# Normalisation of mixers B and C: ScalarE's three operations over two steps, the product on GpSimd

## The reference, cut to what matters

```python
p = jax.nn.softmax(sc, axis=-1)
return jnp.einsum('bhqs,bshd->bqhd', p.astype(v.dtype), v)
```

## Time and profile before

| | |
|---|---|
| time, median of 3 executions | 2663.72 us (2663.42 to 3135.05) |
| profiled execution | 2675.02 us |
| its span on the slowest core (core 0) | 2673.4 us |
| spans of the 8 cores | 2654.1 to 2673.4 us |
| mean granted TensorE clock, core 0 | 0.980 of full speed |
| PE busy | 2548.5 us (95%) |
| DVE busy | 1085.5 us (41%) |
| ACT busy | 1038.7 us (39%) |
| POOL busy | 278.4 us (10%) |
| B and C pairs, layer 0 | about 203 to 579 us |
| B and C pairs, layer 1 | about 1509 to 1876 us |

### The profile page before, as it was taken

How to read it: one execution, slowest core, us unless ns; L and a number is a source line. 1 busy time by engine, 2 the same in 40 slices (tenths; PEclk the granted TensorE clock), 3 DMA queues, 4 the chain that set the end, 5 groups by cost and what they waited for, 6 DMA issues and landing times.

```text
span 2673.4 us, 41394 instructions; the slowest of 8 cores (2654.1 to 2673.4 us)
## 1 busy us (share of the span) xinstructions
PE 2548.5 (95%) x15104; PEld 1234.8 (46%) x15104; DVE 1085.5 (41%) x1612; ACT 1038.7 (39%) x1398; POOL 278.4 (10%) x340
## 2 busy tenths in 40 slices
PE   3889999989999999999999999999999999999997
PEld 1335556544444444444443455565444444444443
DVE  1544434444444414132265444344444462322326
ACT  2567776662223410101154677757222252011012
POOL 2410000000001210000120100000000020000002
PEclk8999999999999999999999999999999999999998
DMA  9304221202234343433331011121122332222214
GB/s 195 66 16 77 49 40 22 63 13 36 42 51 122 65 81 52 71 64 64 87 112 29 16 18 21 22 59 25 24 43 42 75 93 46 40 40 39 41 24 126
DMA packets 66516, 148.01 MB, mean 55 GB/s; under 512 B 6592, under 2 KB 19456, under 8 KB 64272
## 3 DMA queue, kind: packets, MB, share of 16 engines
q0 software_dynamic: 55712, 99.76, 23.5%
q1 hardware_dynamic: 10608, 45.61, 5.1%
HBM read 228.12 MB, written 16.97 MB: 92 GB/s over the span
## 4 chain that ended last, share of the span: by engine, by line
PE 90%; DVE 3%; issue 3%; DMA 2%; ACT 2%; DVEq 0%; POOL 0%; ACTq 0%; POOLq 0%; SPq 0%
PE ps L381 73%; PE ps L379 16%; DMA sb_WS<-wada 1%; DVE sb_OS L410 1%; ACT sb_RD L391 1%; ACT sb_PT L391 1%; DMA sb_XT<-x 0%; DMA sb_WS<-win 0%; DVE sb_W L404 0%; DVE sb_XT L400 0%; DVE sb_TMPF L400 0%; DVE sb_RD L395 0%; ACT sb_HT L391 0%; DVE sb_W L410 0%; DMA sb_WS<-wfi 0%
## 5 line engine op out<-in xcount | busy, mean ns | idle before, releaser
L381 PE MATMUL ps<-sb_HT,sb_WS 128*128 128x512 bf16 (+1 forms) x5760 | 1331.0, 382 | 25.5 <-ACT sb_HT L391 11.9
L381 PEld LDWEIGHTS ps<-sb_HT,sb_WS 128*128 128x128 bf16 (+1 forms) x5760 | 549.6, 98 | 694.9 <-issue 79.8
L391 ACT ACTIVATE sb_TMPF<-ps 128x512 f32<-128x512 f32 x388 | 231.2, 597 | 1127.8 <-PE ps L381 1126.0
L391 ACT ACTIVATE sb_PT<-ps 128x1024 bf16<-128x1024 f32 (+1 forms) x494 | 484.6, 986 | 293.9 <-PE ps L379 288.4
L381 PE MATMUL ps<-sb_W,sb_WS 128*128 128x512 bf16 x1920 | 427.1, 385 | 0.8 <-DVE sb_W L395 0.7
L395 DVE TENSOR_TENSOR sb_W<-ps,sb_TMPF 128x512 bf16<-128x512 f32 x176 | 121.3, 691 | 483.9 <-PE ps L381 471.7
L379 PE MATMUL ps<-sb_PT,sb_W 128*128 128x512 bf16 (+4 forms) x1212 | 281.3, 338 | 36.3 <-ACT sb_PT L391 16.9
L381 PEld LDWEIGHTS ps<-sb_W,sb_WS 128*128 128x128 bf16 x1920 | 189.7, 99 | 233.9 <-issue 30.5
L379 PE MATMUL ps<-sb_W 128*128 128x512 bf16 (+7 forms) x1212 | 256.1, 338 | 0.0
L400 DVE SCALAR_TENSOR_TENSOR sb_XT<-ps,sb_modT,sb_XT 128x512 f32<-128x512 f32 x256 | 186.8, 748 | 161.3 <-PE ps L381 161.0
L410 DVE CAST sb_W<-ps 128x512 bf16<-128x512 f32 (+1 forms) x176 | 121.3, 690 | 250.3 <-PE ps L381 235.0
(11 more groups left out here) (59 smaller groups left out, 1224.8 us busy)
## 6 DMA issues: line engine op xcount, KB each, us to landing
sb_WS<-wada POOLq DMA_DIRECT2D x48, 512.0 KB, 7.7
sb_WS<-wfi POOLq DMA_DIRECT2D x44, 512.0 KB, 5.9
sb_WS<-wmg POOLq DMA_DIRECT2D x48, 384.0 KB, 5.0
sb_XT<-x SPq DMA_DIRECT2D x8, 2048.0 KB, 16.6
sb_WS<-win POOLq DMA_DIRECT2D x60, 256.0 KB, 3.9
sb_WS<-wfo POOLq DMA_DIRECT2D x24, 512.0 KB, 6.0
xs<-sb_XT SPq DMA_DIRECT2D x4, 2048.0 KB, 7.5
sb_XT<-xs SPq DMA_DIRECT2D x4, 2048.0 KB, 16.4
```

Of the source, the lines that this page charges most:

```text
L381: r = e.matmul(o, lhsT=l, rhs=rr, start=st, stop=sp)
L391: return P.op("act", lambda e, o=out, i=in_, f=func, kw=kw: e.activation(out=o, in_=i, func=f, **kw), reads=reads, writes=writes)
```

## The change

The three operations of ScalarE are spread over two calls of run_pend: the first Ln in iteration L+2, the second Ln and the Exp in L+3. The two products follow in L+4 and are done by GpSimd instead of VectorE. The list of pending functions takes one more entry.

```diff
+        def ln(hh):
+            act(RD[HS[hh], ri, :], OS[HS[1 - hh], hh, :], AF.Ln, [osb[hh]], [rdb[ri]])
+
         def st1():
-            for hh in range(2):
-                act(RD[HS[hh], ri, :], OS[HS[1 - hh], hh, :], AF.Ln, [osb[hh]], [rdb[ri]])
+            ln(0)
+
+        def st1b():
+            ln(1)
             act(RD[:, ri, :], RD[:, ri, :], AF.Exp, [], [rdb[ri]], scale=-1.0)
 
         def st2():
             for hh in range(2):
-                tt(out[HS[hh], :], OS[HS[hh], hh, :], RD[HS[hh], ri, :], ALU.mult, [osb[hh], rdb[ri]], wr)
-        return [st0, st1, st2]
+                tt(out[HS[hh], :], OS[HS[hh], hh, :], RD[HS[hh], ri, :], ALU.mult, [osb[hh], rdb[ri]], wr, eng="pool")
+        return [st0, st1, st1b, st2]
...
-                pipe["pend"].append([f[1], f[2]])
+                pipe["pend"].append(f[1:])
```

## The result

The changed kernel takes 1.0064 times the kernel before (95% interval 1.005 to 1.0079), about 17 us more; its three comparable executions took 2679.3, 2682.6 and 2683.0 us, and the prediction was 2665 with a range of 2656 to 2677.

A forecast was written before the change was run, and what follows sets the result against it. TensorE was taken to bound B and C. Boundary terms of +0.7, -0.7 and +0.1 us and -0.25 for four last-C-pair groups sum to +1.2 us, on the 2663.7 us median: 2665 us, range 2656 to 2677.

The forecast's parts named there:

- What bounds it, and where to look: TensorE bounds B and C; only its idle time there is reachable, 30.6 us of waits at most, mainly at pair boundaries.
- the eight boundaries: Three between B pairs and one into the last C pair, per layer: +0.7 each in layer 0; -0.7, -0.7, +0.1, +0.7 in layer 1.
- C pairs with projections: TensorE has no idle time there; forecast unchanged at 41.0 us, lengthening being a sign of a wrong prediction.
- ScalarE: At B boundaries the Exp ends about 0.5 us later; the third step's PV no longer waits 1.04 us.
- VectorE in layer 1: Projection evacuations run before the copies there: -0.7 us at the first two B boundaries, +0.1 at the third.
- GpSimd's price: Each of the 128 products moved to GpSimd takes 1.10 us, with 1.04 and 1.56 as ends.
- The chain from the Exp's end to the PV: At a boundary: two products, each releasing its copy, then the second bank's PV; 3.25 us.
- My sum over these places: Predicted changes at B pair boundaries and into the last C pair, both layers, together: +2.2 us.
- The weight loads: Loads queued behind GpSimd's products go out about 5 us later, hidden by being asked five tiles ahead; cost nothing.
- The last C pair: Inside it, two groups in each layer gain 0.25 us each; the boundary into it costs +0.7 us in each layer.
- the forecast's +0.7 us at a layer 0 boundary: Between B pairs in layer 0, the second bank's PV starts at 262.2 instead of 261.52 us, at three boundaries.
- Rival B: Late GpSimd products delay three-step groups' copies and TensorE at 14 boundaries: +11 us, 2676; slow loads +20 more, 2696; chance 0.12.

The follow-up runs named there:

- the filled kernel: Seven extra throwaway matmuls ahead of the PV that waits, at 8 places, added to the changed kernel; 1.0025 times the kernel before, median 2671.2 us.

## Why the prediction was wrong

**What bounds it, and where to look: right.** All of the difference lies in B and C (17.9 us of 17 measured, within the interval), 15.4 of it at the eight boundaries that the prediction named. C pairs with projections went from 40.94 to 41.15 us; the forecast was no change, and named a longer C pair as a sign of being wrong. These 0.2 us a pair are part of the 2.5 us outside the boundaries, for which the sum had no term.

**ScalarE: right.** The small exponential comes ahead of the second Ln, the Exp ends later by its length, and the wait for exponentials fell from 16.9 to 8.2 us, with none over 0.2 us left at the B boundaries of either layer.

**VectorE in layer 1: right in kind.** With the clock kept up, the first two boundaries of layer 1 are shorter than before by 0.3 us each (forecast 0.7), the third longer by 0.5 (forecast 0.1). The evacuations do run before the copies now.

**GpSimd's price: too low.** "I take 1.10 us, nearest to the first": the row for one tile squared into bf16. It was 1.26, in all 128 instances between 1.25 and 1.27, equal to the shortest for two different tiles. So the two inputs were the better guide to the price than the type of the output. The chain from the Exp's end to the PV was sized at 3.25 us and measured 3.75: 0.32 from the two products, the rest from gaps of 0.14, 0.14 and 0.11 for which I had 0.1, 0.1 and 0.05, and from a copy of 0.69 for which I had 0.65. Over eight boundaries that is 4 us. My sum over these places with it is 2.2 + 4.0 = 6.2; the filled kernel, where the clock stays up, measures 5.5. The mechanism and this sum hold. The weight loads cost nothing, as forecast: TensorE waits for no weights in B and C before or after. The Trainium skill (GPSIMD Engine Reference, Engine selection) has GpSimd at about half of VectorE's speed; the trace is near it, 1.26 / 0.69 = 1.8.

**The last C pair: right within, wrong at its start.** The two groups inside are 0.14 and 0.31 us shorter in each layer (forecast 0.25 each). The way into it costs 1.6 and 1.2 us more with the clock kept up, against 0.7.

**The step that failed: the sum had no term for TensorE's clock.** Every wait was costed at its own length. That length was too short as well: the forecast's +0.7 us at a layer 0 boundary is +0.9 with the clock kept up, and TensorE idles 2.68 us there in place of 1.25. But the larger part is what the engine does after the wait, which the prediction did not ask: the fall of the clock behind seven of eight boundaries costs 9.9 of the 15.4 us on core 4. The rows to ask with were there: in the earlier trace rows the last C pair, with 8 us of waits in 31, has a clock of 0.95 where the B and C stretches have 1.00. That is the trace's own sign that waits can bring the clock down. Its price stands there too: 5% of 31.3 us is 1.6 us. A rival with that mechanism at each of eight boundaries would have given 2665 + 8 x 1.6 = 2678, an estimate, and was not in the list. Rival B had the right place and sign; it was priced by the product's waits alone, and its 2676 set the upper end of the range.

**What stays open.** Why the first boundary of layer 0 keeps its clock with waits of 1.65 and 1.03 us, and why single cores keep theirs at one boundary where the others lose it, no run here tells. Nor does one tell why the B pairs are 0.2 to 0.3 us longer between their second and last groups with the product on GpSimd.

## What to carry to other kernels

When work moves to a slower engine, look for who overwrites its inputs: here a product nobody waited for held a single buffer, and the buffer held the bounding engine. A second buffer turned the same edit from 0.6% slower into 0.45% faster. A wait added on TensorE costs its own length only while the clock stays up; here waits of 2.7 us in all cost another 1.7 us behind them, so see the granted clock after comparable gaps before summing. And test combined edits as such: two parts that cost 0.1% and 0.17% made 0.64% together. Look at every core too: the falls of the clock that one core lacks are in the traces of the others.

## What the runs showed that was not expected

- Extra matmuls made the kernel faster: seven of them (1.67 us) at eight places took 10 us off, since the clock after the gap stayed at 1.00 instead of 0.87 or 0.88.
- The kernel before has as much idle time at a layer 1 boundary (0.97 us for an exponential, then 1.55 and 0.22 for copies) as the changed one (1.59 and 1.03), with a clock of 1.00 over that stretch; there 1.7 us of matmuls lie between the first wait and the second.
- GpSimd's product of two tiles takes 1.26 us at 64 rows into bf16, no less than the shortest at 128 rows into f32 (1.26, median 1.35 of eight); reading one tile twice, at 128 rows into bf16, takes 1.04.
